# A two-block transformer kernel: part of the residual additions of nine norm boundaries moved from VectorE to GpSimd

## The chip, the cores and the metric

The kernel runs on one core of one Trainium2 chip. The core has five engines with instruction streams of their own: TensorE (PE in the rows; its weight loads are PEld), VectorE (DVE), ScalarE (ACT), GpSimd (POOL) and SyncE (SP, which here only starts transfers). They wait for each other through semaphores. The metric is the device time of one execution in microseconds (us).

## The reference, cut to what matters

Two transformer blocks of two layers each work on a residual stream x of 512 tokens by 1024 features; block 2 also carries 256 context tokens. Everything is float32. Each stage ends by adding a normed and scaled result to the stream, and the next begins by norming the stream:

```python
def rmsnorm(x, g):
    y = x * lax.rsqrt(jnp.mean(x * x, axis=-1, keepdims=True) + EPS)
    return y * g
# block 1, each of two layers
x = x + rmsnorm(merged @ w_out, norm_mix_post);  h = rmsnorm(x, norm_mem_pre)
x = x + rmsnorm(memory_cross_attention(h, ...), norm_mem_post);  h = rmsnorm(x, norm_ffn_pre)
x = x + rmsnorm(y_ffn, norm_ffn_post)            # and the next layer: h = rmsnorm(x, norm_mix_pre)
# block 2, each of two layers (the context stream alike in the first)
x = x + gate * rmsnorm(attention_out, g1);  h = modulate(rmsnorm(x, g2))
x = x + gate * rmsnorm(swiglu_out, g3)
```

## The kernel before, in words

Activations lie transposed: a feature tile k holds 128 features on the partitions and the tokens along the free axis. `xres` holds the stream as 8 such tiles. TensorE multiplies float32 as three products of split operands: a tensor is kept as a high part (`hh`, `whi`) rounded by ScalarE and a low part (`hl`, `wlo`), the difference. A weight slab of 8x128 rows by 128 columns is loaded by SP into one of four ring slots (`load`, which waits until the slab four before it has been used), rounded by ScalarE (`head`, L452) and lowered by GpSimd (`tail`, L459: wlo = wraw - whi). Lowering slabs is all that GpSimd does; it waits for `hi_ready` and goes on in the order of the slabs.

A norm boundary lies between two stages. The result y of the stage has been squared and summed, and ScalarE makes 1/rms by a logarithm and an exponential (L527, L530). Then for each k VectorE makes t2 = y[k] * gain * rms (two buffers, k % 2) and xres[k] += t2. There are two forms.

In block 1 (`act_boundary`, `dve_boundary`) the next norm's 1/rms is applied later, so that the high and the low part of h come straight from xres: VectorE's order is t(k), add(k), low(k-1) (L574, L577, L581), ScalarE's is high(k), square(k) (L562, L564), and TensorE sums the square of k (L918 or L547) and multiplies the first slab with tile k (three products, L475 to L477). After k = 7 it goes on with the second slab, 24 products more. Five boundaries have this form: two in each layer, and one between the layers.

In block 2 (`dve_postnorm`, `act_prenorm`) VectorE's order is t(0), t(1), add(0), t(2), add(1) and so on (L770, L780), ScalarE squares (L598), TensorE sums (L520). When all eight are summed ScalarE makes the next 1/rms, and only then `dve_apply` makes h (L620, L635). Four boundaries have this form: the turn from block 1 to block 2 (512 columns), two of 768 columns (512 tokens and 256 of the context; t is two instructions each), and the last with 512. At the turn, TensorE multiplies the context part of three slabs between the sums.

The order on every engine is written out by hand; each engine's program runs in its own order, and a semaphore's counts are kept by `Counts`.

Of the kernel before, what the change touches and what calls it, by code (L numbers as in the profile page):

```python
# [20 lines left out]
ALU = mybir.AluOpType  # L21
# [10 lines left out]
SEQ = 512  # L32
# [14 lines left out]
V1 = K1 + AW  # L47
G1 = V1 + AW
RES = 4
RING = 4  # L50
MW = 512
EPS = 1e-6
# [56 lines left out]
def turns(e, c, n, body):  # L109

    for i in range(n):
        body(e, i)


def two_blocks(nc, A, out):

    with ExitStack() as ctx:  # L117
# [157 lines left out]
        def gain(n):  # L275
            return lambda k: cur[:, n + k:n + k + 1]
# [13 lines left out]
        def sem(name):  # L290
            return ctx.enter_context(nc.semaphore(name))
# [22 lines left out]
        lt_done = sem("out_transposed")  # L314
        lt_out = sem("out_copied")
        x_ready = sem("x_ready")
        sq_ready = sem("sq_ready")
        sq_used = sem("sq_used")
        rstd_ready = sem("rstd_ready")
# [85 lines left out]


        slabs, ada_due = [], []

        def load(e, c, parts, width=P, cols=None):

# [142 lines left out]
                                 xl[:, k, cols], k == 0, k == KT - 1)  # L553
                mm.then_inc(slab_done, 1)

        def act_boundary(e, c, g, half=None):

            for k in range(KT):
                if half and k == KT // 2:
                    half()  # L560
                e.wait_ge(x_ready, c.next(x_ready))
                e.activation(hh[:, k, 0:SEQ], xres[:, k, 0:SEQ], ACT.Copy, scale=g(k)).then_inc(h_hi, 1)  # L562
                e.wait_ge(sq_used, c.next(sq_used))
                e.activation(sq[:, k % 2, 0:SEQ], xres[:, k, 0:SEQ], ACT.Square).then_inc(sq_ready, 1)  # L564
            e.wait_ge(sq_used, c.next(sq_used, KT, view="all"))
            act_rstd(e, c, SEQ)

        def dve_boundary(e, c, g, y=None, G=None):

            if y is not None:  # L570
                e.wait_ge(rstd_ready, c.next(rstd_ready))
            for k in range(KT + 1):
                if k < KT and y is not None:
                    e.scalar_tensor_tensor(out=t2[:, k % 2, 0:SEQ], in0=y[:, k, :], scalar=G(k), in1=ysum[:, 0:SEQ],  # L574
                                           op0=ALU.mult, op1=ALU.mult).then_inc(dve_step, 1)
                    e.wait_ge(dve_step, c.next(dve_step))
                    e.tensor_tensor(xres[:, k, 0:SEQ], xres[:, k, 0:SEQ], t2[:, k % 2, 0:SEQ], ALU.add).then_inc(x_ready, 1)  # L577
                    c.next(x_ready)
                if k:
                    e.wait_ge(h_hi, c.next(h_hi))  # L580
                    e.scalar_tensor_tensor(out=hl[:, k - 1, 0:SEQ], in0=xres[:, k - 1, 0:SEQ], scalar=g(k - 1),  # L581
                                           in1=hh[:, k - 1, 0:SEQ].bitcast(F32), op0=ALU.mult, op1=ALU.subtract)\
                     .then_inc(h_ready, 1)
                    c.next(h_ready)
            e.wait_ge(rstd_ready, c.next(rstd_ready))

        def dve_scaled(e, c, to, s, M=P):
# [5 lines left out]

        def act_prenorm(e, c, T, segs):
            for k in range(KT):
                e.wait_ge(x_ready, c.next(x_ready))
                e.wait_ge(sq_used, c.next(sq_used))
                e.activation(sq[:, k % 2, 0:T], xres[:, k, 0:T], ACT.Square).then_inc(sq_ready, 1)  # L598
            e.wait_ge(sq_used, c.next(sq_used, KT, view="all"))
            act_rstd(e, c, T)  # L600
            act_apply(e, c, hh, range(KT), segs)
# [162 lines left out]
        def dve_postnorm(e, c, T, y, segs, r=rstd):  # L764

            e.wait_ge(rstd_ready, c.next(rstd_ready))

            def scaled(k):
                for a, b, G in segs:
                    e.scalar_tensor_tensor(out=t2[:, k % 2, a:b], in0=y[:, k, a:b], scalar=G(k),  # L770
                                           in1=r[:, a:b], op0=ALU.mult, op1=ALU.mult).then_inc(dve_step, 1)

            scaled(0)
            for k in range(KT):
                e.wait_ge(dve_step, c.next(dve_step, len(segs)))
                if k + 1 < KT:
                    if k:
                        e.wait_ge(x_ready, c.next(x_ready))
                    scaled(k + 1)
                e.tensor_tensor(xres[:, k, 0:T], xres[:, k, 0:T], t2[:, k % 2, 0:T], ALU.add).then_inc(x_ready, 1)  # L780
            e.wait_ge(x_ready, c.next(x_ready, 2))

# [785 lines left out]
        def sp_ffn(e, c, l, up, down):  # L1570
            for p, (u0, n) in enumerate(FF_PARTS):
                def body(e, i):
                    for j in range(2):
                        u = (2 * i + j + u0) * P
                        load(e, c, [(0, P, rows_of(up, l, 0, KT, u))])
                        load(e, c, [(0, P, rows_of(up, l, 0, KT, u + FF))])
                turns(e, c, n // 2, body)
                sp_cols(e, c, down, l, n, u0 * P)

        def sp_cols(e, c, W, l, kt, k0=0):  # L1580
            def body(e, i):
                for j in range(2):
                    load(e, c, [(0, P, rows_of(W, l, k0, kt, (2 * i + j) * P))])
            turns(e, c, KT // 2, body)
# [4 lines left out]
        def _(sp):  # L1589
# [10 lines left out]
            def layer(e, l):  # L1600
                w_in = A["w_in"]
                def heads(j):
                    for base in (Q1, K1, V1):
                        for g in range(3):
                            load(e, c, [(0, P, rows_of(w_in, l, 0, KT, base + g * 256 + j * P))])
                            if len(slabs) == 1:
                                x_rows(3)
                            if j == 0 and base == Q1 and g == 2:
                                e.wait_ge(zone_free, c.next(zone_free))
                                e.dma_start(mask1[:, :, :], A["mask1"]).then_inc(mask_in, 16)  # L1610

                def conv(i):
                    for k in (1, 3, 2):
                        load(e, c, [(0, P, rows_of(w_in, l, 0, KT, k * CW + i * P))])
                heads(0)
                for g in range(4):
                    load(e, c, [(0, P, rows_of(w_in, l, 0, KT, g * PG, PG))], PG)
                conv(0)
                heads(1)
                conv(1)  # L1620
                conv(2)
                load(e, c, [(0, PG, A["pool_w"][bass.ds(l, 1)].rearrange("o g p m -> p (o g) m"))], PG)

                def gates(e, m):
                    for br in range(3):
                        load(e, c, [(0, P, rows_of(w_in, l, 0, KT, m * P + (G1 + br * D)))])
                        if br != 1:
                            ada_due.append((len(slabs) + 1, ADA_BLOCK1 * l + 2 * m + br // 2))
                    load(e, c, [(0, PG, rows_of(A["w_branch_a"], l, 0, 4, m * P, rows=PG))])
                    load(e, c, [(0, P, rows_of(A["w_branch_b"], l, 0, 3, m * P)),  # L1630
                                (3, P, rows_of(A["w_branch_c"], l, 0, 2, m * P))])
                turns(e, c, KT, gates)
                sp_cols(e, c, A["w_out"], l, KT)
                for W, a in (("q", 0), ("kv", 0), ("kv", 4), ("q", 1), ("kv", 1), ("kv", 5), ("q", 2), ("kv", 2), ("kv", 6), ("q", 3),
                             ("kv", 3), ("kv", 7)):
                    load(e, c, [(0, P, rows_of(A["w_m" + W], l, 0, KT, a * P))])
                sp_cols(e, c, A["w_mo"], l, 4)
                sp_ffn(e, c, l, A["w_up"], A["w_down"])
            turns(sp, c, DEPTH, layer)


            ab = A["ab_w_in_2"]
# [19 lines left out]
            load(sp, c, [(0, P, rows_of(ab, 0, 0, KT, 1152))])  # L1662
            turns(sp, c, 3, heads_ab)
            sp_cols(sp, c, A["ab_w_out_2"], 0, KT)
            sp_ffn(sp, c, 0, A["ffn_w13_2"], A["ffn_w2_2"])
            w = A["mla_w_in_2"]
            for j in (0, 3, 4):
                load(sp, c, [(0, P, rows_of(w, 0, 0, KT, j * P))])
# [16 lines left out]
            for h in range(2, C_HEADS):  # L1685
                head_q(h)
                head_kv(h)
            sp_cols(sp, c, A["mla_w_out_2"], 0, KT)
            sp_ffn(sp, c, 1, A["ffn_w13_2"], A["ffn_w2_2"])
            for r in range(4):  # L1690
                sp.wait_ge(lt_out, r + 1)
# [6 lines left out]
        @block.gpsimd  # L1698
        def _(pool):
            c = Counts()  # L1700
            for n in range(len(slabs)):
                tail(pool, c, n)

# [439 lines left out]
        def _(act):  # L2145
# [74 lines left out]

            def layer(e, l):
                e.wait_ge(gains_ready, c.next(gains_ready))
                act_boundary(e, c, gain(0), None if l else lambda: head(e, c))
                act_flow(e, c, [], tiles_1(0), one_each(tiles_1(0)), wide=True, hooks={} if l else with_mem)
                e.activation(ysum[:, 0:SEQ], rstd[:, 0:SEQ], ACT.Square).then_inc(rx2_ready, 1)
                act_flow(e, c, its_1(0), jobs_1(0), ticks_1(0))
# [383 lines left out]
```

## Time and profile before

| | us |
|---|---|
| median of 3 runs | 4000.37 (3993.73 to 4000.42) |
| the profiled execution's own time | 4001.47 |
| its span in the profile | 3999.7 |
| PE, PEld busy | 3786.9, 3183.6 |
| DVE, ACT, POOL busy | 2063.7, 1287.0, 1203.3 |
| mean granted TensorE clock | 0.97 of full |

The span is what the profile's times are counted in; the own time holds the launch around it. Busy time is the sum of instructions on an engine; those of PE overlap in its pipeline, so that its share says that PE nearly always has something in hand and not that it is at its peak. In the rows "x24" is a count, "[0.81 <-DVE xres L577]" says that the engine had been idle for 0.81 us and what ended that.

### The profile page before, as it was taken

The page shows a single profiled execution, that of the slowest core. Times are in us where ns is not written, and L with a number is a line of the kernel's source. Part 1 is how long each engine was busy: PE and PEld are TensorE (multiplying, and loading weights), DVE is VectorE, ACT ScalarE, POOL GpSimd, SP SyncE. Part 2 cuts the span into 40 slices and gives each one's busy share as a digit, 9 for nine tenths or more (in the row PEclk, how much of TensorE's full clock was granted, in tenths as well). Part 3 has the DMA queues.
Part 4 walks back from the last instruction along what each step waited for, and adds up shares of the span by engine and source line. Part 5 has one row for each costly group of instructions (what it writes and reads, how often), then busy time and mean ns, then how long its engine had stood idle before and what let it go on. Part 6 is the DMA issues. An engine that isn't in the chain of part 4 may idle for free. (4 is left out here: it accounts for less than half of the span.)

```text
span 3999.7 us, 49029 instructions
## 1 busy us (share of the span) xinstructions
PE 3786.9 (95%) x19420; PEld 3183.6 (80%) x19420; DVE 2063.7 (52%) x3416; ACT 1287.0 (32%) x2149; POOL 1203.3 (30%) x548
## 2 busy tenths in 40 slices
PE   8999998999999998899989998899999889999999
PEld 6777776888777787688867777799999778877887
DVE  5547646565644773565456665623343566633112
ACT  4332244222433323422234443311111335543223
POOL 2224433444322443244421111122222210123443
PEclk8999999999999999999999997999999999999999
DMA  3224422333212442233321101233332200112332
GB/s 105 64 59 135 125 77 66 116 100 103 82 56 65 126 133 74 74 106 100 111 73 38 28 26 38 69 95 111 95 108 88 62 19 16 28 48 75 94 95 84
DMA packets 544449, 316.71 MB, mean 79 GB/s; under 512 B 35876, under 2 KB 517215, under 8 KB 544223
## 3 DMA queue, kind: packets, MB, share of 16 engines
q1 hardware_dynamic: 525184, 277.39, 23.9%
q10 hardware_dynamic: 19039, 36.19, 2.9%
q8 instruction: 156, 2.56, 0.3%
q14 instruction: 70, 0.57, 0.0%
HBM read 311.44 MB, written 2.10 MB: 78 GB/s over the span
## 5 line engine op out<-in xcount | busy, mean ns | idle before, releaser
L459 POOL TENSOR_TENSOR wlo<-wraw,whi 128x1024 fp32r<-128x1024 f32 (+6 forms) x544 | 1203.1, 2216 | 2774.9 <-ACT whi L452 2774.6
L475 PE MATMUL acc<-hh,whi 128*128 128x512 f32 (+2 forms) x2744 | 1064.1, 388 | 32.1 <-DVE hl L635 24.5
L476 PE MATMUL acc<-hl,whi 128*128 128x512 f32 (+2 forms) x2744 | 1034.7, 377 | 0.0
L477 PE MATMUL acc<-hh,wlo 128*128 128x512 f32 (+2 forms) x2744 | 1034.2, 377 | 0.0
L452 ACT ACTIVATE whi<-wraw 128x1024 fp32r<-128x1024 f32 (+6 forms) x544 | 523.7, 965 | 652.2 <-DMA wraw<-in_w_up 184.9
L475 PEld LDWEIGHTS acc<-hh,whi 128*128 128x128 f32 x2744 | 521.8, 190 | 146.8 <-issue 31.2
L476 PEld LDWEIGHTS acc<-hl,whi 128*128 128x128 f32 x2744 | 521.8, 190 | 91.5 <-issue 12.3
L477 PEld LDWEIGHTS acc<-hh,wlo 128*128 128x128 f32 x2744 | 521.0, 190 | 83.9
L1543 DVE TENSOR_TENSOR t<-acc,sq 128x768 f32<-128x768 f32 (+1 forms) x44 | 36.3, 825 | 444.3 <-PE acc L477 444.3
L475 PE MATMUL ob<-hh,whi 128*128 128x512 f32 (+3 forms) x576 | 214.3, 372 | 6.8 <-DVEq L831 6.6
L475 PE MATMUL acc<-act1h,whi 128*128 128x512 f32 x528 | 209.7, 397 | 1.4 <-DVE act1l L1551 1.4
L476 PE MATMUL acc<-act1l,whi 128*128 128x512 f32 x528 | 208.8, 395 | 0.0
L477 PE MATMUL acc<-act1h,wlo 128*128 128x512 f32 x528 | 208.8, 395 | 0.0
L477 PE MATMUL ob<-hh,wlo 128*128 128x512 f32 (+3 forms) x576 | 205.3, 356 | 0.0
L476 PE MATMUL ob<-hl,whi 128*128 128x512 f32 (+3 forms) x576 | 205.1, 356 | 0.0
L697 DVE TENSOR_SCALAR y<-acc 128x512 f32<-128x512 f32 (+1 forms) x80 | 59.6, 745 | 260.7 <-PE acc L477 260.4
L1005 ACT ACTIVATE t<-acc,small 128x768 f32<-128x768 f32 (+1 forms) x160 | 116.5, 729 | 235.7 <-DVE small L1105 235.7
L1100 DVE TENSOR_REDUCE small<-acc 128x1 f32<-128x768 f32 (+1 forms) x160 | 118.7, 742 | 91.8 <-PE acc L863 85.8
L1472 ACT ACTIVATE sq<-acc 128x768 f32<-128x768 f32 (+1 forms) x44 | 31.0, 705 | 388.7 <-PE acc L477 388.7
L699 DVE TENSOR_TENSOR y<-acc,y 128x512 f32<-128x512 f32 (+1 forms) x64 | 48.5, 758 | 203.5 <-PE acc L477 202.8
L590 DVE TENSOR_TENSOR zf<-acc,rstd 128x512 f32<-128x512 f32 x88 | 60.9, 692 | 161.6 <-PE acc L477 160.6
L475 PEld LDWEIGHTS ob<-hh,whi 128*128 128x128 f32 (+1 forms) x576 | 108.8, 189 | 26.6 <-issue 11.9
(412 smaller groups left out, 6232.4 us busy)
## 6 DMA issues: line engine op xcount, KB each, us to landing
wraw<-in_ffn_w SPq DMA_DIRECT2D x120, 512.0 KB, 3.8
wraw<-in_w_in SPq DMA_DIRECT2D x102, 512.0 KB, 3.9
wraw<-in_w_up SPq DMA_DIRECT2D x88, 512.0 KB, 3.8
ada_w<-in_ada_w ACTq DMA_DIRECT2D x64, 512.0 KB, 4.1
ada_w<-in_ada_w SPq DMA_DIRECT2D x32, 512.0 KB, 4.2
wraw<-in_w_down SPq DMA_DIRECT2D x32, 512.0 KB, 4.0
wraw<-in_w_out SPq DMA_DIRECT2D x16, 512.0 KB, 4.1
wraw<-in_w_mkv SPq DMA_DIRECT2D x16, 512.0 KB, 4.0
```

The source lines that it names most:

```text
L452: e.activation(whi[0:rows, s, a:b, 0:w], wraw[0:rows, s, a:b, 0:w], ACT.Copy).then_inc(hi_ready, 1)
L459: e.tensor_tensor(wlo[0:rows, s, a:b, 0:w], wraw[0:rows, s, a:b, 0:w], whi[0:rows, s, a:b, 0:w].bitcast(F32), ALU.subtract).then_inc(lo_re ...
L475: e.matmul(o, wh, xh, start=first, stop=False)
L476: e.matmul(o, wh, xl, start=False, stop=False)
L477: return e.matmul(o, wl, xh, start=False, stop=last)
L590: e.tensor_tensor(to, one(s)[0:M, :], rstd[0:M, 0:SEQ], ALU.mult).then_inc(dve_step, 1)
L697: e.tensor_scalar(ym, bank(s, T), 1.0, None, ALU.mult).then_inc(kept, 1)
L699: e.tensor_tensor(ym, bank(s, T), ym, ALU.add).then_inc(kept, 1)
L1005: e.activation(to, src, ACT.Exp, bias=bias, scale=-1.0 if t["mask"] is not None else t["scale"], accum_out=small[:, den:den + 1]).then_inc ...
L1100: st(e.tensor_reduce(mx, S, AX_X, ALU.max))
L1472: e.activation(v3(sq[:, j, 0:T], T), bank(s, T), ACT.Silu).then_inc(act_step, 1)
L1543: e.tensor_tensor(v3(w, T), bank(s1, T), v3(sq[:, j, 0:T], T), ALU.mult)\
```

## The change

For k = 1 to 7 in the five boundaries of block 1, and for k = 1, 3, 5, 7 in the four others, the addition xres[k] += t2 is issued on GpSimd (`pool_adds`). VectorE keeps t, the other additions and the low parts. Two semaphores are new: `t_scaled` (t is there) and `x_added` (the addition is done). VectorE's t(k), which overwrites the buffer of t(k-2), waits for the addition of k-2. SP's program, which only builds the list of slabs, notes behind which slab GpSimd makes the additions of a boundary: after it has lowered the first two slabs of the next stage (three at the turn).

```diff
@@ -47,6 +47,8 @@
 V1 = K1 + AW
 G1 = V1 + AW
 RES = 4
+LATER = (1, 2, 3, 4, 5, 6, 7)
+ODD = (1, 3, 5, 7)
 RING = 4
 MW = 512
 EPS = 1e-6
...
@@ -314,6 +316,7 @@
         lt_done = sem("out_transposed")
         lt_out = sem("out_copied")
         x_ready = sem("x_ready")
+        t_scaled, x_added = sem("t_scaled"), sem("x_added")
         sq_ready = sem("sq_ready")
         sq_used = sem("sq_used")
         rstd_ready = sem("rstd_ready")
...
@@ -405,6 +408,16 @@
 
 
         slabs, ada_due = [], []
+        stage_ends = {}
+
+        def ends_here(T, tiles, waits, ahead=2):
+            stage_ends[len(slabs) + ahead] = (T, tiles, waits)
+
+        def pool_adds(e, c, T, tiles, waits):
+
+            for k in tiles:
+                e.wait_ge(t_scaled, c.next(t_scaled, waits))
+                e.tensor_tensor(xres[:, k, 0:T], xres[:, k, 0:T], t2[:, k % 2, 0:T], ALU.add).then_inc(x_added, 1)
 
         def load(e, c, parts, width=P, cols=None):
 
...
@@ -553,12 +566,13 @@
                                  xl[:, k, cols], k == 0, k == KT - 1)
                 mm.then_inc(slab_done, 1)
 
-        def act_boundary(e, c, g, half=None):
+        def act_boundary(e, c, g, half=None, added=LATER):
 
             for k in range(KT):
                 if half and k == KT // 2:
                     half()
-                e.wait_ge(x_ready, c.next(x_ready))
+                done = x_added if k in added else x_ready
+                e.wait_ge(done, c.next(done))
                 e.activation(hh[:, k, 0:SEQ], xres[:, k, 0:SEQ], ACT.Copy, scale=g(k)).then_inc(h_hi, 1)
                 e.wait_ge(sq_used, c.next(sq_used))
                 e.activation(sq[:, k % 2, 0:SEQ], xres[:, k, 0:SEQ], ACT.Square).then_inc(sq_ready, 1)
...
@@ -571,8 +585,13 @@
                 e.wait_ge(rstd_ready, c.next(rstd_ready))
             for k in range(KT + 1):
                 if k < KT and y is not None:
+                    if k == 2:
+                        e.wait_ge(x_ready, c.at(x_ready, 0))
+                    if k >= 3:
+                        e.wait_ge(x_added, c.next(x_added))
                     e.scalar_tensor_tensor(out=t2[:, k % 2, 0:SEQ], in0=y[:, k, :], scalar=G(k), in1=ysum[:, 0:SEQ],
-                                           op0=ALU.mult, op1=ALU.mult).then_inc(dve_step, 1)
+                                           op0=ALU.mult, op1=ALU.mult).then_inc(t_scaled if k else dve_step, 1)
+                if k == 0 and y is not None:
                     e.wait_ge(dve_step, c.next(dve_step))
                     e.tensor_tensor(xres[:, k, 0:SEQ], xres[:, k, 0:SEQ], t2[:, k % 2, 0:SEQ], ALU.add).then_inc(x_ready, 1)
                     c.next(x_ready)
...
@@ -582,6 +601,8 @@
                                            in1=hh[:, k - 1, 0:SEQ].bitcast(F32), op0=ALU.mult, op1=ALU.subtract)\
                      .then_inc(h_ready, 1)
                     c.next(h_ready)
+            if y is not None:
+                e.wait_ge(x_added, c.next(x_added, 2))
             e.wait_ge(rstd_ready, c.next(rstd_ready))
 
         def dve_scaled(e, c, to, s, M=P):
...
@@ -593,7 +614,8 @@
 
         def act_prenorm(e, c, T, segs):
             for k in range(KT):
-                e.wait_ge(x_ready, c.next(x_ready))
+                done = x_added if k in ODD else x_ready
+                e.wait_ge(done, c.next(done))
                 e.wait_ge(sq_used, c.next(sq_used))
                 e.activation(sq[:, k % 2, 0:T], xres[:, k, 0:T], ACT.Square).then_inc(sq_ready, 1)
             e.wait_ge(sq_used, c.next(sq_used, KT, view="all"))
...
@@ -768,17 +790,20 @@
             def scaled(k):
                 for a, b, G in segs:
                     e.scalar_tensor_tensor(out=t2[:, k % 2, a:b], in0=y[:, k, a:b], scalar=G(k),
-                                           in1=r[:, a:b], op0=ALU.mult, op1=ALU.mult).then_inc(dve_step, 1)
+                                           in1=r[:, a:b], op0=ALU.mult, op1=ALU.mult).then_inc(t_scaled if k in ODD else dve_step, 1)
 
             scaled(0)
             for k in range(KT):
-                e.wait_ge(dve_step, c.next(dve_step, len(segs)))
                 if k + 1 < KT:
                     if k:
-                        e.wait_ge(x_ready, c.next(x_ready))
+                        done = x_added if k - 1 in ODD else x_ready
+                        e.wait_ge(done, c.next(done))
                     scaled(k + 1)
-                e.tensor_tensor(xres[:, k, 0:T], xres[:, k, 0:T], t2[:, k % 2, 0:T], ALU.add).then_inc(x_ready, 1)
-            e.wait_ge(x_ready, c.next(x_ready, 2))
+                if k not in ODD:
+                    e.wait_ge(dve_step, c.next(dve_step, len(segs)))
+                    e.tensor_tensor(xres[:, k, 0:T], xres[:, k, 0:T], t2[:, k % 2, 0:T], ALU.add).then_inc(x_ready, 1)
+            e.wait_ge(x_ready, c.next(x_ready))
+            e.wait_ge(x_added, c.next(x_added))
 
 
 
...
@@ -1631,12 +1656,17 @@
                                 (3, P, rows_of(A["w_branch_c"], l, 0, 2, m * P))])
                 turns(e, c, KT, gates)
                 sp_cols(e, c, A["w_out"], l, KT)
+                ends_here(SEQ, LATER, 1)
                 for W, a in (("q", 0), ("kv", 0), ("kv", 4), ("q", 1), ("kv", 1), ("kv", 5), ("q", 2), ("kv", 2), ("kv", 6), ("q", 3),
                              ("kv", 3), ("kv", 7)):
                     load(e, c, [(0, P, rows_of(A["w_m" + W], l, 0, KT, a * P))])
                 sp_cols(e, c, A["w_mo"], l, 4)
+                ends_here(SEQ, LATER, 1)
                 sp_ffn(e, c, l, A["w_up"], A["w_down"])
+                if l < DEPTH - 1:
+                    ends_here(SEQ, LATER, 1)
             turns(sp, c, DEPTH, layer)
+            ends_here(SEQ, ODD, 1, ahead=3)
 
 
             ab = A["ab_w_in_2"]
...
@@ -1662,7 +1692,9 @@
             load(sp, c, [(0, P, rows_of(ab, 0, 0, KT, 1152))])
             turns(sp, c, 3, heads_ab)
             sp_cols(sp, c, A["ab_w_out_2"], 0, KT)
+            ends_here(TC, ODD, 2)
             sp_ffn(sp, c, 0, A["ffn_w13_2"], A["ffn_w2_2"])
+            ends_here(TC, ODD, 2)
             w = A["mla_w_in_2"]
             for j in (0, 3, 4):
                 load(sp, c, [(0, P, rows_of(w, 0, 0, KT, j * P))])
...
@@ -1686,6 +1718,7 @@
                 head_q(h)
                 head_kv(h)
             sp_cols(sp, c, A["mla_w_out_2"], 0, KT)
+            ends_here(SEQ, ODD, 1)
             sp_ffn(sp, c, 1, A["ffn_w13_2"], A["ffn_w2_2"])
             for r in range(4):
                 sp.wait_ge(lt_out, r + 1)
...
@@ -1700,6 +1733,8 @@
             c = Counts()
             for n in range(len(slabs)):
                 tail(pool, c, n)
+                if n + 1 in stage_ends:
+                    pool_adds(pool, c, *stage_ends[n + 1])
 
 
 
...
@@ -2220,7 +2255,7 @@
 
             def layer(e, l):
                 e.wait_ge(gains_ready, c.next(gains_ready))
-                act_boundary(e, c, gain(0), None if l else lambda: head(e, c))
+                act_boundary(e, c, gain(0), None if l else lambda: head(e, c), added=LATER if l else ())
                 act_flow(e, c, [], tiles_1(0), one_each(tiles_1(0)), wide=True, hooks={} if l else with_mem)
                 e.activation(ysum[:, 0:SEQ], rstd[:, 0:SEQ], ACT.Square).then_inc(rx2_ready, 1)
                 act_flow(e, c, its_1(0), jobs_1(0), ticks_1(0))
```

## Rows read from the trace of the kernel before

**Rows 1.** Page, part 1: busy us (share), instructions by engine
```profile
PE 3786.9 (95%) x19420; PEld 3183.6 (80%) x19420; DVE 2063.7 (52%) x3416; ACT 1287.0 (32%) x2149; POOL 1203.3 (30%) x548
```

**Rows 2.** Stretches of two boundaries: busy us by engine, granted clock, DMA
```profile
533.00:552.00 19.00, 15.52 (x46) 8.81 (x47) 16.30 (x24) 11.05 (x19) 0.00 (x0) 0.91 0.01 1
...
2542.00:2575.00 33.00, 19.80 (x51) 11.70 (x52) 27.03 (x45) 14.04 (x20) 0.00 (x0) 0.79 0.00 0
```

**Rows 3.** Timeline of the first block 1 boundary: start us, us, engine, line, operation
```profile
533.14 0.75 DVE L574 SCALAR_TENSOR_TENSOR t<-y,cur,ysum 128x512 f32<-128x512 f32 x1 [3.35 <-ACT ysum L530]
533.92 0.69 DVE L577 TENSOR_TENSOR xres<-xres,t 128x512 f32<-128x512 f32 x1
534.53 0.74 DVE L574 SCALAR_TENSOR_TENSOR t<-y,cur,ysum 128x512 f32<-128x512 f32 x1
534.65 0.72 ACT L562 ACTIVATE hh<-xres,cur 128x512 fp32r<-128x512 f32 x1 [1.54 <-DVE xres L577]
...
538.17 0.63 PE L476 MATMUL acc<-hl,whi 128*128 128x512 f32 x1
...
538.60 0.63 PE L477 MATMUL acc<-hh,wlo 128*128 128x512 f32 x1
...
544.78 0.74 DVE L574 SCALAR_TENSOR_TENSOR t<-y,cur,ysum 128x512 f32<-128x512 f32 x1
...
546.83 0.74 DVE L574 SCALAR_TENSOR_TENSOR t<-y,cur,ysum 128x512 f32<-128x512 f32 x1
...
548.22 1.63 DVE L581 SCALAR_TENSOR_TENSOR hl<-xres,cur,hh 128x512 fp32r<-128x512 f32 x2
...
550.28 0.79 PE L475 MATMUL acc<-hh,whi 128*128 128x512 f32 x1
...
550.91 0.39 PE L476 MATMUL acc<-hl,whi 128*128 128x512 f32 x1
...
551.14 0.40 PE L477 MATMUL acc<-hh,wlo 128*128 128x512 f32 x1
```

**Rows 4.** Timeline of VectorE, first boundary with 768 columns
```profile
2543.03 2.33 DVE L770 SCALAR_TENSOR_TENSOR t<-y,cur,rstd 128x512 f32<-128x512 f32 x4 [0.24 <-DVE rope_s L1383]
2545.27 0.95 DVE L780 TENSOR_TENSOR xres<-xres,t 128x768 f32<-128x768 f32 x1
...
2558.01 1.82 DVE L780 TENSOR_TENSOR xres<-xres,t 128x768 f32<-128x768 f32 x2
```

**Rows 5.** Timeline of VectorE, last boundary
```profile
3591.50 1.54 DVE L770 SCALAR_TENSOR_TENSOR t<-y,cur,rstd 128x512 f32<-128x512 f32 x2 [3.34 <-ACT rstd L530]
...
3601.72 1.28 DVE L780 TENSOR_TENSOR xres<-xres,t 128x512 f32<-128x512 f32 x2
```

**Rows 6.** Timeline of the boundary at the turn from block 1 to block 2
```profile
2080.15 1.29 DVE L780 TENSOR_TENSOR xres<-xres,t 128x512 f32<-128x512 f32 x2
...
2091.46 0.69 ACT L527 ACTIVATE rstd<-pt,small 128x512 f32<-128x512 f32 x1 [3.87 <-PE pt L520]
```

**Rows 7.** GpSimd's groups by shape: count | busy us, mean ns | idle before
```profile
L459 POOL TENSOR_TENSOR wlo<-wraw,whi 128x768 fp32r<-128x768 f32 x41 | 75.9, 1854 | 182.2 <-ACT whi L452 182.2
...
L459 POOL TENSOR_TENSOR wlo<-wraw,whi 128x512 fp32r<-128x512 f32 x16 | 20.6, 1287 | 59.8 <-ACT whi L452 59.8
```

**Rows 8.** Timeline, GpSimd beside VectorE in the gates of block 1
```profile
300.77 0.75 DVE L1383 SCALAR_TENSOR_TENSOR ada_s<-ada_w,scT,ada_s 128x512 f32<-128x512 f32 x1
...
301.27 1.40 POOL L459 TENSOR_TENSOR wlo<-wraw,whi 96x512 fp32r<-96x512 f32 x1 [3.07 <-ACT whi L452]
...
301.44 1.79 DVE L1383 SCALAR_TENSOR_TENSOR sq<-ada_w,scT,sq 128x512 f32<-128x512 f32 x1
```

**Rows 9.** Line L590: count, duration ns min/median/max, one operand in PSUM
```profile
L590 DVE TENSOR_TENSOR zf<-acc,rstd x88: 691/692/693, 672.5 to 2028.4; 128x512 f32<-128x512 f32 x88
```

**Rows 10.** Timeline of GpSimd around the first block 1 boundary
```profile
525.96 2.40 POOL L459 TENSOR_TENSOR wlo<-wraw,whi 128x1024 fp32r<-128x1024 f32 x1 [4.98 <-ACT whi L452]
553.35 9.90 POOL L459 TENSOR_TENSOR wlo<-wraw,whi 128x1024 fp32r<-128x1024 f32 x4 [24.99 <-ACT whi L452]
```


## The prediction

> **What bounds the kernel now.** I read the page's busy shares first [rows 1]: PE has work in hand for 95% of the span, VectorE for 52%, GpSimd for 30%. So time is lost or won only where PE waits, and the question is what PE waits for in a norm boundary. The windows over the boundaries come next [rows 2]: in 19.0 us of a block 1 boundary VectorE is busy for 16.30 and PE for 15.52 at a granted clock of 0.91; in the 33 us around a boundary of 768 columns VectorE is busy for 27.03 and PE for 19.80; GpSimd does nothing in either. VectorE sets the pace there, and the change takes work from it. Whether that pays depends on what GpSimd does to VectorE when both run, so the third view is the timeline: of a block 1 boundary [rows 3], of the block 2 boundaries [rows 4 to 6], and below of a place where the two engines meet.
>
> In the block 1 boundary VectorE repeats t, add, low every 2.05 us (544.78 to 546.83), with hardly a gap. It starts at 533.14 and its last low part ends at 549.85 (548.22 + 1.63), 16.71 us later; PE multiplies tile 7 at 550.28 and then has the second slab, which waits for nothing [rows 3]. What delays the last low part therefore delays everything behind it. All five boundaries of this form repeat that pattern. In block 2 the eight t and add pairs of 768 columns take 16.80 us (2543.03 to 2558.01 + 1.82) and those of the last boundary 11.50 (3591.50 to 3601.72 + 1.28), and the chain of squares, sums and 1/rms hangs on the last addition [rows 4, 5]. At the turn it doesn't: the last addition ends at 2081.44, and ScalarE's logarithm starts only at 2091.46, released by PE [rows 6], which multiplies context tiles there.
>
> **The price of an addition on GpSimd.** The trace before has no such addition. The nearest rows are GpSimd's subtractions of the same shapes with two inputs in SBUF, 1.29 us at 512 columns and 1.85 at 768 [rows 7], against 0.69 and 0.95 for VectorE's addition [rows 3, 4]. I take these; below there is only the hope that a plain float32 result is cheaper than the rounded one.
>
> **What the two engines do to each other.** VectorE's L1383 runs until 301.52 [rows 8], and GpSimd's instruction is issued at 301.27: it ends at 302.67, 1.15 us behind VectorE's end. The next L1383 starts at 301.44, in the same queue with no wait, and takes 1.79 us where the one before took 0.75: it ends 0.56 us after GpSimd. So each is held until the other is through, GpSimd got its turn between two VectorE instructions that were back to back, and what overlaps is only the start-up: 0.14 of GpSimd's 1.29, 0.19 of VectorE's 0.75. L590, which reads one operand from PSUM, took 691 to 693 ns in all its 88 runs [rows 9], so it isn't held. In the boundaries t reads y and 1/rms, the additions xres and t2, the low part xres and hh: all two from SBUF, all of the kind that is held.
>
> The Trainium skill's page "SBUF — State Buffer", section "Who interferes with whom", speaks against this change by the same mechanism: a VectorE instruction with two SBUF inputs and a GpSimd instruction that reads SBUF exclude each other, and the one issued first keeps the shared ports for its whole length. By the rule the work is not split but put in a row, and the sum is the one below; without it, the first rival. The trace agrees [rows 8].
>
> **Block 1, one boundary, followed** (0 is the start of t(0); a hop between engines is 0.04 (VectorE's end at 534.61, ScalarE at 534.65) [rows 3], a VectorE instruction behind another adds its length less 0.08, a high part on ScalarE is 0.72). t(0) ends at 0.75, add(0) at 1.47, t(1) at 2.13. GpSimd's add(1) starts at 2.17, just ahead of low(0) (ready 2.27), and ends at 3.46; low(0), held, at 4.02; t(2) 4.68; low(1) 5.34, its high part was ready at 4.22. add(2), asked for at 4.72, gets its turn at 5.34 and ends at 6.49; t(3), held, 7.05. Now low(2) waits for its high part until 7.29, so add(3) goes first, 7.09 to 8.38; low(2) 8.94; t(4) 9.60; low(3) 10.26; add(4) 11.41; t(5) 11.97. Two tiles take 4.92 us (7.05 to 11.97) instead of 4.10. On so: t(7) 16.89, add(7) 18.22, low(6) 18.78, high(7) 18.98, low(7) 19.76. Against 16.71 that is +3.05, and nothing covers it; five boundaries, **+15.3**. ScalarE keeps up (additions end at least 1.9 us apart), PE waits longer. The first additions run while nothing else is asked of GpSimd: its last lowering ends at 528.4, and the next, at 553.35, waits for ScalarE's high part, which comes behind the boundary in ScalarE's own order [rows 10]. So what is queued behind the waiting additions loses nothing, SP's refills neither.
>
> Bounds of this term: if no start-up overlaps, each of seven additions costs 0.14 + 0.18 more, +2.2 a boundary, 11 in all. If the engines don't hold each other at all, the same walk gives low(7) at 15.59, 1.1 less than before: even then little is gained, for t(k+1) waits behind low(k-1), and that for add(k-1) and its high part, 3.53 us for two tiles.
>
> **Block 2.** With 768 columns: t(0), t(1) end at 2.33, add(0) at 3.19 (2545.27 + 0.95), add(1) gets its turn there and ends 1.85 - 0.14 later, at 4.90. Then a pair of tiles costs 1.71 for GpSimd, 0.56 for the held half of t, 1.57 for the other three t instructions (2.24 less 0.67) and 0.86 for VectorE's addition: 4.70, before 4.25 (12.74 over six tiles, 2545.27 to 2558.01). add(7) ends at 4.90 + 3 x 4.70 = 19.0, against 16.80: +2.2, two boundaries **+4.4**. With 512 columns: add(1) ends at 2.14 + 1.15 = 3.29; a pair costs 1.15 + 0.56 + 0.67 + 0.60 = 2.98 against 2.92; add(7) at 12.2 against 11.50: **+0.7**, in the last boundary. At the turn the 10 us between the last addition and the logarithm cover it: **0** (0.7 without that cover). Without overlap of start-ups these twelve additions cost 4 more; with no holding the two forms end 2.8 and 2.5 earlier than before, 8.1 in all.
>
> The new waits: t(k) waits for add(k-2), always through by then in the walk above; SP's part is bookkeeping of the program text.
>
> **Sum.** 15.3 + 4.4 + 0.7 = +20.4 on the profiled execution's 4001.5, which stood 1.1 above the median of the runs. From the median 4000.4: **4021 us**.
>
> **Rivals.** (a) The engines run side by side, because the holding is something particular to the place seen [rows 8]. For it: GpSimd is idle here and VectorE is the bound. Against it: it is seen for an instruction of the same kind, and VectorE's unmoved time only with a PSUM operand [rows 9]. 5 x -1.1 - 8.1 = -13.6: 3987 us. It decides from the point where a VectorE instruction beside a GpSimd one keeps its 0.75 us. (b) Holding is real, but the plain addition is cheaper than the lowering. Break-even is where two additions save the 0.82 us that two tiles lose, at about 0.9 us each; then 4000 us. The Trainium skill ("GPSIMD Engine Reference", section "3.1 Elementwise — side-by-side cycle accounting") counts about 2.6 cycles an element whatever the type, an estimate of 1.1 us of streaming, which would leave little room for (b); the trace's slope from 512 to 768 columns is 2.2 ns an element [rows 7]. (c) The PE clock. At the lower of its two levels (1.2 GHz) products follow each other every 0.43 us (538.17, 538.60), at 2.4 GHz every 0.23 (550.91, 551.14) [rows 3]; it was low when PE came out of its wait for the boundary's first tile, and the longer waits between tiles may keep it low into the second slab. At worst 24 x 0.20 = 4.8 a boundary, 24 in all: 4045; half of that 4033. For it: clock 0.91 in the 19 us of a boundary. Against: PE waits in every tile already, and the level rose all the same. That the change doesn't do what it says (GpSimd's additions placed behind a lowering that comes later) I rule out [rows 10]: both slabs of the first wave are lowered before the boundary begins.
>
> **Chances.** Forecast 0.66 (4014 to 4036, from a luckier order of turns to no overlap), (a) 0.10, (b) or another cover that leaves it within the measurement 0.12, (c) 0.12. A difference of 0.2%, 8 us, is about what can be told from none. Slower 0.78, same 0.12, faster 0.10. The range leaves out (a) and the far end of (c): 4003 to 4038.
>
> **What would show it.** In the profile after, VectorE's L574, L581 and L770 equivalents with a mean well above 0.75 us, the long ones ending 0.56 behind GpSimd; additions on GpSimd of 1.3 us, or 1.2 measured from the end of the VectorE instruction in front; 4.9 us for two tiles in block 1; the turn unchanged. If those VectorE instructions keep 0.75 us, the forecast is wrong by its main step; if the additions take 0.9 us, by the price; if PE's granted clock in the second slabs is at the lower level, it is too small.

## The result and the profile after

The changed kernel takes 4022.3 us (median of 4 runs, 4015.9 to 4026.0) against 3997.4 for the kernel before on the same chips (3993.7 to 4000.4): ratio 1.0061, interval 1.0048 to 1.0074, slower by about 24 us. Forecast were 4021 us and +20.4. The two profiled executions stand 18.6 us apart (4020.06 and 4001.47).

Part 1 of the page after, beside [rows 1]:

```profile
PE 3789.2 (94%) x19420; PEld 3176.3 (79%) x19420; DVE 2078.8 (52%) x3365; ACT 1287.0 (32%) x2149; POOL 1286.7 (32%) x599
```

VectorE has lost 51 additions and is busy for longer than the 2063.7 us of before. The timeline of the first block 1 boundary after (start us, us, engine, line, operation) answers to [rows 3]:

```profile
533.39 0.75 DVE L592 SCALAR_TENSOR_TENSOR t<-y,cur,ysum 128x512 f32<-128x512 f32 x1 [3.35 <-ACT ysum L543]
...
534.79 0.74 DVE L592 SCALAR_TENSOR_TENSOR t<-y,cur,ysum 128x512 f32<-128x512 f32 x1
...
535.61 1.27 POOL L420 TENSOR_TENSOR xres<-xres,t 128x512 f32<-128x512 f32 x1 [7.00 <-DVE t L592]
535.66 1.77 DVE L600 SCALAR_TENSOR_TENSOR hl<-xres,cur,hh 128x512 fp32r<-128x512 f32 x1
...
538.01 0.74 DVE L600 SCALAR_TENSOR_TENSOR hl<-xres,cur,hh 128x512 fp32r<-128x512 f32 x1
...
538.17 1.71 POOL L420 TENSOR_TENSOR xres<-xres,t 128x512 f32<-128x512 f32 x1 [1.29 <-DVE t L592]
...
538.67 1.75 DVE L592 SCALAR_TENSOR_TENSOR t<-y,cur,ysum 128x512 f32<-128x512 f32 x1
...
540.51 1.28 POOL L420 TENSOR_TENSOR xres<-xres,t 128x512 f32<-128x512 f32 x1 [0.63 <-DVE t L592]
...
540.67 1.67 DVE L600 SCALAR_TENSOR_TENSOR hl<-xres,cur,hh 128x512 fp32r<-128x512 f32 x1 [0.24 <-ACT hh L576]
...
543.59 1.77 DVE L592 SCALAR_TENSOR_TENSOR t<-y,cur,ysum 128x512 f32<-128x512 f32 x1
...
548.49 1.77 DVE L592 SCALAR_TENSOR_TENSOR t<-y,cur,ysum 128x512 f32<-128x512 f32 x1
...
551.65 0.72 ACT L576 ACTIVATE hh<-xres,cur 128x512 fp32r<-128x512 f32 x1 [0.66 <-POOL xres L420]
...
552.40 0.75 DVE L600 SCALAR_TENSOR_TENSOR hl<-xres,cur,hh 128x512 fp32r<-128x512 f32 x1 [0.24 <-ACT hh L576]
...
554.60 0.28 PE L488 MATMUL acc<-hh,whi 128*128 128x256 f32 x1
```

GpSimd's add(1) starts at 535.61, 0.05 ahead of low(0), which takes 1.77 us and ends at 537.43, 0.55 behind GpSimd. add(2) is asked for while low(1) runs and takes 1.71; t(3), issued in its shadow, takes 1.75. From then on one t or low part in two is a long one. Two tiles take 4.90 us (t(5) at 543.59 to t(7) at 548.49), where they took 4.10, and the last low part ends at 553.15, 19.76 us after the start (before 16.71). TensorE begins the second slab at 554.60, 21.21 us after the start; before that was 18.24 (533.14 to 551.38). GpSimd's two new groups, the answer to [rows 7] (count, busy us, mean ns, idle before):

```profile
L420 POOL TENSOR_TENSOR xres<-xres,t 128x512 f32<-128x512 f32 x43 | 64.4, 1498 | 72.7 <-DVE t L592 57.4 <-DVE t L792 15.4
...
L420 POOL TENSOR_TENSOR xres<-xres,t 128x768 f32<-128x768 f32 x8 | 19.6, 2455 | 33.8 <-DVE t L792 33.8
```

The means hold the waiting inside: the undisturbed one is 1.27 us. In the boundary of 768 columns, the answer to [rows 4]:

```profile
2561.29 0.95 DVE L804 TENSOR_TENSOR xres<-xres,t 128x768 f32<-128x768 f32 x1
2561.45 2.45 POOL L420 TENSOR_TENSOR xres<-xres,t 128x768 f32<-128x768 f32 x1 [12.32 <-DVE t L792]
...
2562.27 3.63 DVE L792 SCALAR_TENSOR_TENSOR t<-y,cur,rstd 128x512 f32<-128x512 f32 x4
...
2565.83 0.94 DVE L804 TENSOR_TENSOR xres<-xres,t 128x768 f32<-128x768 f32 x1
...
2565.98 2.46 POOL L420 TENSOR_TENSOR xres<-xres,t 128x768 f32<-128x768 f32 x1 [2.08 <-DVE t L792]
```

add(1) ends at 2563.90, 1.66 behind VectorE's addition, and four t instructions take 3.63 us instead of 2.33. A pair costs 4.54 us (2561.29 to 2565.83), before 4.25.

Measured in all nine places, from the first t to the last low part in block 1 and to the logarithm in block 2 (the instruction of L527, from the timelines; "order only" is the experiment e1 below, in which block 2 has the new order of instructions but no work on GpSimd):

| us | before | after | order only |
|---|---|---|---|
| five boundaries of block 1, each | 16.71 | 19.75 | |
| the turn | 22.39 | 21.57 | 21.57 |
| 768 columns, two, each | 19.75 | 20.88 | 19.20 |
| the last | 13.64 | 13.83 | 13.09 |
| sum of the nine | 159.1 | 175.9 | |
| the stretches between them | 3840.6 | 3842.1 | 3836.5 |

For one order of instructions the boundaries are the same to 0.1 us in every profiled execution (block 1's to 0.03), except the turn: it took 21.1 to 22.0 us in the four executions that have the changed kernel's block 2 (this one, e0, e2, e10). The stretches between the boundaries vary too. Over the executions of this study in which they do the same work they add up to 3832 to 3848 us, and the first 535 us alone vary by 8. So single executions say little on 5 us, and the boundaries' lengths say nearly all.

### The profile page after: what moved, and what is told of

Its sections match the earlier page's. It is cut to its first block and busy times, and to the rows that moved or that the text cites. A ratio compares the mean times of both kernels' runs of the same rounds, so it can differ in the third digit from the quotient of the medians.

```text
span 4018.0 us, 49008 instructions
## 1 busy us (share of the span) xinstructions
PE 3789.2 (94%) x19420; PEld 3176.3 (79%) x19420; DVE 2078.8 (52%) x3365; ACT 1287.0 (32%) x2149; POOL 1286.7 (32%) x599
```

## The experiments

**The changed kernel again (e0).** No edit.

> The changed kernel again, unaltered, beside the kernel before on one chip. Theory H (VectorE and GpSimd hold each other when both read from SBUF): the two profiled executions differ by 18.6 us, of which the boundaries account for five times 3.04 in block 1 and about 1.7 in block 2; so +17 to +21 us, ratio 1.0043 to 1.0052. Rival R (something outside the boundaries is slower as well, since the runs so far differ by 24 us): +23 us or more, ratio 1.0058 or more, and then the profile must show stretches between boundaries that are longer.

Ratio 1.0052 (1.0039 to 1.0066), +21 us: at the upper end of H, with an interval that reaches into R. This interval and that of the first comparison both hold 20 us. The profile decides. Its boundaries are those of the table to 0.1 us. Its span is 4.5 us longer than the first profile's, of which 4.3 lie in one stretch of 493 us between two boundaries that no edit touches. No stretch outside the boundaries is slower in both executions by more than it varies elsewhere.

**Block 1 alone, block 2 alone (e1, e2).**

```diff
-ODD = (1, 3, 5, 7)          # e1: block 2 adds on VectorE
+ODD = ()
-LATER = (1, 2, 3, 4, 5, 6, 7)   # e2: block 1 as before
+LATER = ()
```

(with the waits to match)

> Only the five block 1 boundaries have their additions on GpSimd (k = 1 to 7); the four others are as before. H: each boundary takes 19.75 us from the first scaling to the last low part as in the changed kernel, 16.71 before, so +15.2 us (ratio 1.0038). R (the time is lost in new waits and hops, spread over all nine): 5 of 9 boundaries and 35 of 51 additions, +12.8 us of 18.6.

> Only the four block 2 boundaries have their odd additions on GpSimd; block 1 is as before. H: +1.1 us for each boundary of 768 columns, +0.2 for the last, -0.8 to 0 at the turn, so +1.6 to +2.4 us, not to be told from none (ratio 1.0004 to 1.0006). R: +5.8 us (16 of 51 additions).

e1: ratio 1.0035 (1.0022 to 1.0048), +14 us. The interval holds both expectations; the trace separates them. Block 1's boundaries are 19.75, as H has it. But block 2's, with no addition on GpSimd, came out shorter than before (the column "order only"), by 2.5 us in all. In the last three boundaries (1.7 us) the cause stands in the change: the wait for t(k) was moved behind t(k+1), so that two t instructions run back to back. I had read over it. So H should have said +13.5 instead of +15.2. The other 0.8 us lie at the turn, and are not the order's (below). e2: ratio 1.0014 (1.0005 to 1.0023), +5.6 us, close to R, where the boundaries' own sum is +1.2; the rest is within what the stretches between vary, and the interval reaches from the upper end of H past R. The windows over the turn (us, busy us of PE, PEld, DVE, ACT, POOL, granted clock, DMA); before, after, e1, e10 (block 2 as in the changed kernel) and e4 (the order of the kernel before, 1/rms in PSUM):

```profile
2069.00:2091.50 22.50, 18.54 (x88) 13.23 (x88) 11.69 (x16) 5.12 (x10) 1.13 (x1) 0.78 0.21 66
```

```profile
2084.84:2106.40 21.56, 17.80 (x88) 12.54 (x88) 11.62 (x12) 5.08 (x9) 7.77 (x5) 0.84 0.22 69
```

```profile
2077.50:2099.00 21.50, 17.67 (x88) 12.54 (x88) 11.60 (x16) 5.15 (x9) 1.21 (x1) 0.84 0.22 69
```

```profile
2080.10:2102.10 22.00, 18.27 (x88) 12.97 (x88) 11.60 (x12) 5.06 (x9) 7.67 (x5) 0.79 0.21 67
```

```profile
2063.20:2084.20 21.00, 18.00 (x88) 12.70 (x88) 10.79 (x16) 5.04 (x8) 1.17 (x1) 0.84 0.23 71
```

After and e1 are alike, with GpSimd and without; before, the granted clock was 0.78 instead of 0.84, and the stretch 0.8 us longer. The order of instructions doesn't decide it: e10 with the new order and a clock of 0.79 takes 22.00 us, e4 with the old order and 0.84 takes 20.98. The turn's -0.8 us is therefore not put down to the change.

**t that reads 1/rms from PSUM (e3, and e4 as its control).** Otherwise the changed kernel, and the kernel before:

```diff
+        RMS = [ob[1][:, 0:SEQ], ob[0][:, 0:CTX]]
-                act_postnorm(e, c, SEQ, ysum[:, 0:SEQ])
+                act_postnorm(e, c, SEQ, RMS[0])
-... scalar=G(k), in1=ysum[:, 0:SEQ], ...
+... scalar=G(k), in1=RMS[0], ...
```

> The changed kernel with one operand moved: ScalarE writes the 1/rms of every boundary to a PSUM bank that is idle there, so that VectorE's t = y * gain * rms has one input in SBUF instead of two. Work, waits and order are otherwise the same (for 768 columns the exponential is two instructions, about 0.4 us more). H: t is held no more and keeps its 0.75 us; only the low parts and VectorE's own additions are still held. By the same walk with t unheld, two tiles of block 1 take 4.2 us instead of 4.9, a boundary 17.4 us instead of 19.75 (before 16.71); a pair of 768 columns 3.7 instead of 4.5 (before 4.25). In all about 0 to +3 us against the kernel before, ratio 1.000 to 1.001, 17 us or so less than the changed kernel. R (hops, waits and the slower engine cost the time, not the holding): the long t instructions of 1.75 us stay, and the time stays within 3 us of the changed kernel's.

> Control: the kernel before with 1/rms in PSUM and nothing on GpSimd. H: nothing is held there anyway, so t keeps 0.74 us, a block 1 boundary 16.7 us, and the boundaries of 768 columns gain nothing (the exponential is two instructions, 0 to 0.4 us more). Rival: t is faster from PSUM by itself (the gain of the experiment before came from that): t under 0.70 us and a boundary under 16.4.

e3: ratio 0.9999 (0.9989 to 1.0010): with one operand moved, the kernel is back at the time of before. Its timeline in block 1:

```profile
540.79 1.00 DVE L602 SCALAR_TENSOR_TENSOR hl<-xres,cur,hh 128x512 fp32r<-128x512 f32 x1 [1.26 <-ACT hh L578]
...
541.72 0.73 DVE L594 SCALAR_TENSOR_TENSOR t<-y,cur,ob 128x512 f32<-128x512 f32 x1
...
542.37 0.74 DVE L602 SCALAR_TENSOR_TENSOR hl<-xres,cur,hh 128x512 fp32r<-128x512 f32 x1
542.53 0.39 PE L491 MATMUL acc<-hl,whi 128*128 128x512 f32 x1
...
543.04 0.74 DVE L594 SCALAR_TENSOR_TENSOR t<-y,cur,ob 128x512 f32<-128x512 f32 x1
...
547.27 0.73 DVE L594 SCALAR_TENSOR_TENSOR t<-y,cur,ob 128x512 f32<-128x512 f32 x1
```

GpSimd is at work from 542.53 on (two additions in 2.95 us), and t(5) at 543.04 takes 0.74. Two tiles take 4.23 us (543.04 to 547.27; expected 4.2), a boundary 17.72 (expected 17.4), those of 768 columns 18.4. So block 1's boundaries still cost 1.0 us each (their low parts are held as before, up to 1.76 us), and block 2's, 5.2 us shorter in sum than before (1.9 of them at the turn), make up for it. The t of block 1 in both kernels (count, ns min/median/max), after and e3:

```profile
L592 DVE SCALAR_TENSOR_TENSOR t<-y,cur,ysum x32: 737/748/1770, 533.4 to 1698.7; 128x512 f32<-128x512 f32 x32
```

```profile
L594 DVE SCALAR_TENSOR_TENSOR t<-y,cur,ob x32: 733/735/748, 533.5 to 1697.0; 128x512 f32<-128x512 f32 x32
```

The control e4 shows that PSUM gives next to nothing by itself in these boundaries: t takes 0.74 us, block 1's boundaries 16.67, those of 768 columns 19.67. It is the holding that went. As a whole e4 took 3990.8 us against 4003.5 for the kernel before, one run each; its boundaries are 1.8 us shorter, and the rest lies in the stretches between. One run doesn't tell whether 1/rms in PSUM gains anything there.

**What holds (e6, e7).** GpSimd writes a constant, or copies t2, where it added:

```diff
-                e.tensor_tensor(xres[:, k, 0:T], xres[:, k, 0:T], t2[:, k % 2, 0:T], ALU.add).then_inc(x_added, 1)
+                e.memset(xres[:, k, 0:T], 1.0).then_inc(x_added, 1)                                       # e6
+                e.tensor_scalar(xres[:, k, 0:T], t2[:, k % 2, 0:T], 1.0, None, ALU.mult).then_inc(x_added, 1)   # e7
```

> The changed kernel, in which GpSimd writes a constant to xres[k] instead of adding t2 to it, behind the same waits: the residual additions that had been moved are left out, so its time stands only for the holding. It reads nothing from SBUF. H (they hold each other over the reading of SBUF): no t or low part is longer than 0.76 us, however long GpSimd takes. Rival (any GpSimd instruction in SBUF holds VectorE): some of them end 0.5 to 0.6 us behind a GpSimd end.

> The changed kernel, in which GpSimd copies t2 to xres[k] (one input from SBUF) instead of adding: the moved additions are left out. H: reading one operand is enough to hold, so t and low parts that meet it are lengthened by its length less about 0.2 us and end 0.56 us behind it, and a boundary is shorter than 19.75 only by what the copy is shorter than the addition's 1.29 us, seven times. Rival (it takes two inputs on GpSimd's side): no VectorE instruction longer than 0.76 us.

Both leave the moved additions out (one run each, 3995.9 and 4002.8 us, against one of 4003.5 for the kernel before), so only the lengths of their instructions are read. e6, the timeline and block 1's low parts:

```profile
542.01 0.74 DVE L600 SCALAR_TENSOR_TENSOR hl<-xres,cur,hh 128x512 fp32r<-128x512 f32 x1
542.15 0.53 POOL L420 MEMSET xres<- 128x512 f32 x1 [0.94 <-DVE t L592]
```

```profile
L600 DVE SCALAR_TENSOR_TENSOR hl<-xres,cur,hh x40: 743/751/754, 537.9 to 1680.1; 128x512 fp32r<-128x512 f32 x40
```

In block 1 GpSimd's constants fall beside low parts, 30 of the 40, and beside no t. A low part has two inputs in SBUF like t, and none is longer than 0.754 us: a GpSimd instruction that reads nothing doesn't hold. (One t of e6 is long, 1.62 us, the first of the turn: it runs beside a lowering, which reads two.) e7:

```profile
538.13 1.49 POOL L420 TENSOR_SCALAR xres<-t 128x512 f32<-128x512 f32 x1 [7.02 <-DVE t L592]
538.17 1.12 DVE L600 SCALAR_TENSOR_TENSOR hl<-xres,cur,hh 128x512 fp32r<-128x512 f32 x1
...
540.03 1.49 POOL L420 TENSOR_SCALAR xres<-t 128x512 f32<-128x512 f32 x1 [0.41 <-DVE t L592]
...
540.41 0.78 DVE L600 SCALAR_TENSOR_TENSOR hl<-xres,cur,hh 128x512 fp32r<-128x512 f32 x1 [0.46 <-ACT hh L576]
```

Neither expectation came true. The copy takes 1.49 us, longer than the addition, and low(0), issued 0.04 behind it, takes 1.12 us and not the 2.0 that it would if held until the copy's end (539.62 + 0.55 - 538.17): it ends at 539.29, so it was let in about 0.6 us after the copy began (539.29 less the 0.55 that a held one takes to end). The next one, issued 0.38 behind, takes 0.78. So a one-input instruction holds only for about the first 0.6 us of its 1.49, presumably while it reads; that GpSimd's reading is over by then was not measured.

**Fewer additions in block 1 (e10).**

```diff
-LATER = (1, 2, 3, 4, 5, 6, 7)
+LATER = (1, 3, 5, 7)
```

(with VectorE adding the even ones, and the waits to match)

> The changed kernel with fewer additions on GpSimd in block 1: k = 1, 3, 5, 7 instead of 1 to 7. H, walked as in the prediction: two tiles take 4.40 us (before 4.10, changed 4.92) and a boundary 18.9 us (16.71, 19.75). R (a fixed price for every addition moved, 3.05 us for seven): 1.75 us for four, a boundary 18.45.

```profile
534.82 0.75 DVE L592 SCALAR_TENSOR_TENSOR t<-y,cur,ysum 128x512 f32<-128x512 f32 x1 [3.35 <-ACT ysum L543]
...
542.14 1.76 DVE L592 SCALAR_TENSOR_TENSOR t<-y,cur,ysum 128x512 f32<-128x512 f32 x1
...
546.54 1.75 DVE L592 SCALAR_TENSOR_TENSOR t<-y,cur,ysum 128x512 f32<-128x512 f32 x1
...
552.93 0.75 DVE L600 SCALAR_TENSOR_TENSOR hl<-xres,cur,hh 128x512 fp32r<-128x512 f32 x1 [1.92 <-ACT hh L576]
```

Two tiles take 4.40 us (542.14 to 546.54) and a boundary 18.86 (534.82 to 553.68): the walk, 4.40 and 18.9, and not a fixed price per addition (18.45). One run, 4018.4 us.

**Order alone, and two combinations (e8, e9, e5).** VectorE's loop in block 1 in e8 and e9, partly in words; e8 has in block 2 the changed kernel's order with all additions on VectorE; e5 and e9 have block 2 as the changed kernel, with 1/rms in PSUM:

```diff
+            scaled(0)
             for k in range(KT + 1):
-                    t(k) ; wait for it ; add(k)
+                    scaled(k + 1) ; wait for t(k) ; add(k)
                 ... low(k - 1)
```

> The kernel before with no work on GpSimd, only VectorE's order changed. Block 1: t(k+1) is issued ahead of add(k), so that no addition follows the t it needs at once (0.12 us of waiting a tile). Block 2: the wait for t(k) stands behind t(k+1), as in the changed kernel. Theory H2 (the changed kernel holds a small gain that is not GpSimd's: the moved wait): the boundaries of block 2 take 19.2, 19.2 and 13.1 us to the logarithm (before 19.75, 19.75, 13.64) as in the kernel with block 1 alone on GpSimd, and the turn 21.6 (before 22.39), -2.5 us; a tile of block 1 costs 0.66 + 0.66 + 0.61 = 1.93 instead of 2.05, a boundary 15.75 instead of 16.71, -4.8. In all -7 us, ratio 0.998. Rival: in block 1 the wait only moves to the high part of ScalarE, a boundary stays at 16.7, and the gain is -2.5 us, not to be told from none.

> That order in block 1 on VectorE alone, and in block 2 the odd additions on GpSimd with 1/rms in PSUM, so that t isn't held. H: 15.75 a boundary in block 1; block 2 as in the experiment with 1/rms in PSUM (18.4, 18.4, 13.0 us and 20.5 at the turn): -4.8 - 5.2 = -10 us, ratio 0.9975; the fastest of all. Rival: the same as the kernel with the order alone (ratio 0.998), if what is won inside the boundaries of block 2 is given back in the stage behind.

> Block 1's boundaries as before, except that 1/rms lies in PSUM; block 2 has its odd additions on GpSimd and 1/rms in PSUM. H: 16.7 us a boundary in block 1, block 2 -5.2 us: ratio 0.9987. Rival R (hops and waits of the moved additions cost what they cost in the same kernel with 1/rms in SBUF): +1.2 us inside the boundaries, ratio 1.0003 or more.

e8: ratio 0.9999 (0.9990 to 1.0008), no gain where 7 us were expected. Block 2's boundaries came as expected (19.19, 19.20, 13.08 and 21.56 at the turn); the interval allows for those 2.5 us, not for 7. VectorE's part of a block 1 boundary did shrink, to 15.84 us, and yet next to nothing came of it. The first boundary, and of the second the start of its second slab:

```profile
530.20 1.41 DVE L573 SCALAR_TENSOR_TENSOR t<-y,cur,ysum 128x512 f32<-128x512 f32 x2 [3.35 <-ACT ysum L530]
...
544.43 1.62 DVE L589 SCALAR_TENSOR_TENSOR hl<-xres,cur,hh 128x512 fp32r<-128x512 f32 x2
...
545.42 1.02 PE L926 MATMUL pt<-sq,ones 128*128 128x512 f32 x2
...
546.98 1.02 PE L926 MATMUL pt<-sq,ones 128*128 128x512 f32 x2
...
548.54 0.28 PE L475 MATMUL acc<-hh,whi 128*128 128x256 f32 x1
...
668.91 0.40 PE L475 MATMUL acc<-hh,whi 128*128 128x512 f32 x1
```

The last low part ends at 546.05, but TensorE sums the last squares at 546.98 and begins the second slab at 548.54, 18.34 us after the start: as before (18.24). From 539.20 on it does a tile every 1.55 us (545.42 to 546.98) with no wait for VectorE: its first tiles ran at the lower level of its clock (products 0.42 us apart, at 535.91 and 536.33), and that backlog it doesn't work off. The order itself adds to the backlog, as the first product comes 4.49 us after the start instead of 3.82. In the five boundaries the second slab begins after 18.33, 17.67, 18.70, 18.31 and 17.67 us (before four times 18.24 or 18.25, and 18.38). That is 0.7 us less in all, where 4.4 were taken off VectorE. Before the change TensorE had only just caught up: from tile 4, 5 or 6 on it waits for each low part of VectorE's but the last (the product follows 0.39 us behind), and in the fifth boundary it doesn't wait at all. So what is taken off VectorE here is worth little, and what is put on is paid in full. How much TensorE could have used, e6 shows best: there the first product isn't delayed, and the second slab began 17.77, 17.06, 17.00, 17.08 and 16.97 us after the start, 0.5 to 1.4 sooner than before, with the last low parts 2.1 to 2.9 sooner.

e9: 0.9983 (0.9974 to 0.9991); e5: 0.9977 (0.9968 to 0.9987), 3991.1 us (median of 9) against 4000.7. For e9 0.9975 and the fastest of all were expected; it isn't the fastest. The two intervals overlap, which fits: e9 adds to e5 only the order that was worth little. In e5 the pair of 768 columns:

```profile
2542.81 0.95 DVE L805 TENSOR_TENSOR xres<-xres,t 128x768 f32<-128x768 f32 x1
2542.97 2.46 POOL L422 TENSOR_TENSOR xres<-xres,t 128x768 f32<-128x768 f32 x1 [1.25 <-DVE t L793]
...
2543.80 1.14 DVE L793 SCALAR_TENSOR_TENSOR t<-y,cur,ob 128x512 f32<-128x512 f32 x2
...
2545.47 1.14 DVE L793 SCALAR_TENSOR_TENSOR t<-y,cur,ob 128x512 f32<-128x512 f32 x2 [0.53 <-POOL xres L422]
...
2546.52 0.95 DVE L805 TENSOR_TENSOR xres<-xres,t 128x768 f32<-128x768 f32 x1
```

A pair takes 3.71 us (2542.81 to 2546.52): t at 2543.80 runs in its 1.14 us beside GpSimd. What remains is t(k) waiting 0.53 us for add(k-2), and the boundary is 18.38 us (before 19.75, order only 19.20). e5 is faster than the kernel before and the changed one. Its boundaries account for 5.6 us: 2.7 in those of 768 columns, 0.6 in the last, 0.2 in block 1, and 2.1 at the turn, which also varies without an edit. The rest of the 9 is of the size that the stretches between vary, and could also be PSUM's, as e4 was fast too: that GpSimd's help is worth 9 us isn't shown.

## Why the prediction was right

**The main step, that the two engines hold each other in the boundaries, is shown** by e3 (one operand out of SBUF, and block 1's longest t falls from 1.77 us to 0.75), its control e4, and e6 (no reading by GpSimd, no long low part). Rival (a), that they run side by side, is out. The trace of before already held the case inside a boundary, which I had passed over: the first t of the turn, beside a lowering, takes 1.62 us and ends 0.55 behind it.

```profile
2067.79 2.34 POOL L459 TENSOR_TENSOR wlo<-wraw,whi 128x1024 fp32r<-128x1024 f32 x1 [1.85 <-ACT whi L452]
2069.06 1.62 DVE L770 SCALAR_TENSOR_TENSOR t<-y,cur,ysum 128x512 f32<-128x512 f32 x1 [1.78 <-ACT ysum L530]
```

The Trainium skill's page "SBUF — State Buffer", section "Who interferes with whom", agrees in who meets whom: e6 writes without reading and doesn't hold, e3's t with one SBUF input isn't held. Where the same page, in its section "Summary: rules for kernel authors", has the second one blocked until the first finishes, the additions agree and e7's one-input copy differs: 0.6 of 1.49 us.

**Block 1, +15.3 us**: measured 5 x 3.04 = 15.2. The walk gave 19.76 a boundary, the trace 19.73 to 19.76; two tiles 4.92, measured 4.90 to 4.92; TensorE's second slab begins 2.97 later, so the whole of it is exposed. What the walk lacked is a term for TensorE, which e8 shows to be nearly the limit itself. It didn't matter for a loss; for rival (a), 1.1 us less a boundary, it is close to all that TensorE could have taken up (0.5 to 1.4 us in e6).

**Block 2, +5.1 us**: right in size for the wrong starting point. Against the same order on VectorE the last addition comes 2.11, 2.11 and 1.00 us later (18.35, 18.35, 11.95 against 16.24, 16.24, 10.95 in e1), 5.2 in all. Against the kernel before it comes only 1.55, 1.55 and 0.45 later, as the moved wait gives 0.56 a boundary back, a step of the change that the prediction left out. At the logarithm another 0.43 (0.26 in the last) is missing, since the square of tile 6 is done while GpSimd adds tile 7. Net +2.4. **The turn, 0**: -0.8, which follows neither GpSimd nor the order; executions with the same instructions there differ by 0.9.

**Price of an addition**, 1.29 and 1.85 us by the lowering: 1.26 to 1.28 undisturbed; at 768 columns 1.66 behind a VectorE instruction, taken as 1.71. Rival (b) is out. **The clock**, rival (c): the second slab after runs at the higher level; out. The sum inside the boundaries is +16.8 where 20.4 were forecast; that the runs' medians came out at +24 and +21, so near the forecast, is in part luck: block 2's term was 2.7 too large, and the stretches between, which vary by more than that, put it back. Why those vary between executions was not looked into further.

## What to carry to other kernels

Before work is moved from VectorE to GpSimd, list which instructions of the two will overlap and how many inputs each reads from SBUF: two on VectorE and any addition on GpSimd is not parallel work but a queue, in which GpSimd's longer instruction replaces the shorter. An input in PSUM takes VectorE's instruction out of that queue. And ask what the next engine would do with the time: here TensorE could have used about 1 us a boundary.

## What the runs showed that was not expected

GpSimd's one-input multiplication by 1.0 takes 1.49 us at 128x512, its two-input addition 1.27, its constant 0.53. It holds VectorE for about 0.6 us of its 1.49, the addition for all of its length. Two t instructions without a wait between them follow each other after 0.67 us (e8); an addition that waits for the t in front of it starts 0.79 us after that t. Block 1's boundaries repeat to 0.03 us from execution to execution while whole stages differ by 4 to 5 us.
